# 32 bytes allocated ahead of the arena in a one-layer decoder kernel: every tile behind it moves up by 32 bytes

## What is computed

```python
mod = silu(c) @ w_mod + b_mod                       # 2048 x 12288: six rows or columns of shifts, scales, gates
h = rms_norm(x, norm1_g) * (1 + sc1) + sh1
z = h @ w_in                                        # 2048 x 5296, split into heads, gates, conv channels
o_fox = fox_attention(...)                          # 12 heads of 64
o_nsa = nsa_attention(...)                          # 12 heads, three branches
o_conv = conformer_conv(...)                        # 512 channels, 31 taps
x = x + g1 * (concat(o_fox, o_nsa, o_conv) @ w_out) # 2048 x 2048
h = rms_norm(x, norm2_g) * (1 + sc2) + sh2
x = x + g2 * (relu(h @ w_mlp1) ** 2 @ w_mlp2)       # 2048 x 8192 and 8192 x 2048
return rms_norm(x, final_g)
```

## The kernel before, in words

| tiles | first address | over a multiple of 64 |
|---|---|---|
| `raw`, `w_hi`, `w_lo` | 16,512 | 0 |
| `mod_raw`, `acc`; in them `t_hi`, `t_lo`, `acc_hi`, and `s_hi`, `s_lo` 1 and 2 | 82,048 | 0 |
| small constants and columns (`ident` to `cmp_r`) | 114,816 | 0 or 32 |
| `arena` (68.5 KB): `x_a`, `z_t`, `val_f`, `conv_y`, `mix_f`, `score`, `fox_hi`, `conv_hi`, `x2`, `xn2`, `u_hi`, `u_lo`, `y`, `relu`, `late_raw` | 122,272 | 32 |
| `hold` (32 KB): `act`, `bias_t`, `nsa_hi`, `first_raw` 4 to 6, `end_hi`, `end_lo` | 192,416 | 32 |
| `early3` (4 KB), and at its place `conv_b`, `ones_r`, `s_hi` 0, `s_lo` 0 | 225,184 | 32 |

## Time and profile before

### The profile page before, as it was taken

How to read it: one execution, slowest core, us unless ns; L and a number is a source line. 1 busy time by engine, 2 the same in 40 slices (tenths; PEclk the granted TensorE clock), 3 DMA queues, 4 the chain that set the end, 5 groups by cost and what they waited for, 6 DMA issues and landing times.

```text
span 1172.2 us, 17842 instructions
## 1 busy us (share of the span) xinstructions
PE 1134.7 (97%) x7087; PEld 1005.2 (86%) x7087; DVE 983.7 (84%) x1182; ACT 641.5 (55%) x936; POOL 23.6 (2%) x40
## 2 busy tenths in 40 slices
PE   4999999999999999999999999999999999999996
PEld 4899989999887778999788888888888888888885
DVE  5998989988997988997887788987778987878774
ACT  6655458877775546544454445554455544445452
POOL 1000000100000000010000000000000000000000
PEclk6999999999999999999999999999999999999999
DMA  9999998878966897985657675657674667666451
GB/s 372 420 420 420 421 409 310 255 205 281 358 227 249 301 304 292 401 351 183 210 186 266 240 282 180 215 187 277 238 270 176 218 202 263 251 231 262 152 180 72
DMA packets 48322, 314.65 MB, mean 268 GB/s; under 512 B 6572, under 2 KB 8440, under 8 KB 11768
## 3 DMA queue, kind: packets, MB, share of 16 engines
q1 hardware_dynamic: 44592, 305.72, 70.1%
q0 software_dynamic: 1760, 5.26, 2.4%
q10 hardware_dynamic: 1896, 2.64, 0.8%
HBM read 305.20 MB, written 4.21 MB: 264 GB/s over the span
## 4 chain that ended last, share of the span: by engine, by line
PE 76%; DVE 11%; DMA 5%; ACT 4%; issue 3%; SPq 0%; ACTq 0%; DVEq 0%
PE quad L1285 15%; PE quad L1299 10%; PE quad L1300 10%; PE quad L1301 10%; PE quad L1287 8%; PE quad L1275 5%; PE quad L1276 5%; PE quad L1277 5%; DMA first_raw<-in_w_mod 3%; DVE w_lo L1850 3%; PE quad L1346 2%; PE quad L1345 2%; PE quad L1347 2%; DVE mod_raw L1857 2%; DMA mod_raw<-in_w_mod 2%
## 5 line engine op out<-in xcount | busy, mean ns | idle before, releaser
L893 ACT ACTIVATE w_hi<-raw 128x1024 fp32r<-128x1024 f32 (+1 forms) x342 | 355.4, 1044 | 304.9 <-PE quad L1301 115.9
L1850 DVE TENSOR_TENSOR w_lo<-raw,w_hi 128x1024 fp32r<-128x1024 f32 (+1 forms) x342 | 408.3, 1204 | 112.4 <-ACT w_hi L893 110.4
L1285 PE MATMUL quad<-act,w_hi 128*128 128x512 f32 x768 | 266.4, 390 | 0.0
L1275 PE MATMUL quad<-act,w_hi 128*128 128x256 f32 x760 | 215.2, 283 | 6.0 <-DVE w_lo L1850 3.9
L1287 PE MATMUL quad<-act,w_lo 128*128 128x256 f32 x768 | 216.6, 282 | 0.0
L1276 PE MATMUL quad<-act,w_hi 128*128 128x256 f32 x760 | 213.1, 280 | 0.0
L1277 PE MATMUL quad<-act,w_lo 128*128 128x256 f32 x760 | 213.1, 280 | 0.0
L1285 PEld LDWEIGHTS quad<-act,w_hi 128*128 128x128 f32 x768 | 144.2, 188 | 30.2
L1275 PEld LDWEIGHTS quad<-act,w_hi 128*128 128x128 f32 x760 | 144.1, 190 | 8.7 <-issue 4.6
L1299 PE MATMUL quad<-w_hi,u_hi 128*128 128x512 f32 x376 | 148.8, 396 | 0.6 <-DVE u_lo L2307 0.6
L1301 PE MATMUL quad<-w_hi,u_lo 128*128 128x512 f32 x376 | 148.7, 396 | 0.0
(11 more groups left out here) (371 smaller groups left out, 1715.6 us busy)
## 6 DMA issues: line engine op xcount, KB each, us to landing
raw<-in_w_main SPq DMA_DIRECT2D x184, 1024.0 KB, 5.0
mod_raw<-in_w_mod SPq DMA_DIRECT2D x67, 1024.0 KB, 7.2
first_raw<-in_w_mod SPq DMA_DIRECT2D x14, 1024.0 KB, 15.3
late_raw<-in_w_mod SPq DMA_DIRECT2D x10, 1024.0 KB, 7.9
acc<-in_w_mod SPq DMA_DIRECT2D x4, 1024.0 KB, 12.5
conv_b<-conv_q POOLq DMA_DIRECT2D x8, 512.0 KB, 5.2
x_a<-in_x SPq DMA_DIRECT2D x2, 1024.0 KB, 7.2
x_scratch<-x SPq DMA_DIRECT2D x1, 2048.0 KB, 11.7
```

The source lines that it names most:

```text
L893: A(dst[:, 0:2 * width], block_half(raw, j, width), ACT.Copy).then_inc(hi_done, 1)
L1275: mm(out, hi, act_hi[:, k, :], start=begin and m % 2 == 0, stop=False, skip_group_check=True)
L1285: mm(out, w_hi[j % 4][:, cols], act_both[:, k, :, :].rearrange("p h t -> p (h t)"), start=begin, stop=False, skip_group_check=True)
L1850: TTn(lo[:, 0:2 * width], block_half(raw, j, width), hi[:, 0:2 * width].bitcast(f32), ALU.subtract)\
```

## The change

One tile of 32 bytes per partition is allocated between the small tiles and the arena. Nothing reads or writes it. `arena_at` and `hold_at` are worked out from the allocator's position behind both, and so move with them; `early3` follows.

```diff
         cmp_r = sb("cmp_r", [P, TT * NNSA])
 
 
+        shift = sb("shift", [P, 8])
         arena = sb("arena", [P, ARENA // 4])
         hold = sb("hold", [P, 2 * KT * S])
         arena_at, hold_at = nc.sbuf_base - ARENA - 8 * KT * S, nc.sbuf_base - 8 * KT * S
```

## The result

| kernel | median us | runs | ratio to before | 95% interval |
|---|---|---|---|---|
| before | 1173.41 | 1172.91 to 1174.53, 4 | | |
| changed | 1179.8 | 1176.86 to 1180.97, 4 | 1.0047 | 1.0035 to 1.0058 |
| changed, a second set | 1179.07 | 1178.31 to 1181.45, 5 | 1.0049 | 1.0035 to 1.0062 |

In the second set the kernel before had a median of 1174.06 us. The changed kernel is slower by 5 to 6.4 us; 1181.0 us was forecast. All medians in this document are over executions at the full clock; one execution, the profiled one of e6_arena_minus32, had a granted clock of 0.556 and took 1878.78 us.

A forecast was written before the change was run, and what follows sets the result against it. The prediction took TensorE to bound the kernel. Terms 3.8 + 4.8 + 0.3 - 1.0 = 7.9 us, with the 1172.2 us profiled span and 0.9 us to the median, gave 1181.0 us; 8-in-10 range 1171 to 1186 us.

The forecast's parts named there:

- four signs: Profile after: L1285 at about 396 ns, its pairs 351 to 354, L1275 118 to 119 a matmul, `end_hi` rows at 396.
- What bounds the kernel: Whole kernel: TensorE, busy 97% of the span, hardly waits, so nearly all its lost pace delays the end.
- The pace goes by the moving operand: at a remainder of 32 it is 227 ns: Back-to-back matmuls: moving address 32 over a multiple of 64 gives 227 ns for 512 columns, 0 gives 230 to 233.5.
- The four pairs of remainders: Trace before: bytes over a multiple of 64 for (moving, stationary): (32, 0), (0, 32), (32, 32) and (0, 0).
- the (0, 0) row: Four unread 512-column products, both operands at multiples of 64: read as 230 ns a matmul, to some 3 ns.
- `merged_rows`, +3.8 us: 768 pairs of 512 and 256 columns: from 346.7 to 351.6 ns, 3.8 us more.
- `feature_rows`, +4.8 us less 1.0 hidden: 2280 matmuls of 256 columns: from 116.7 to 118.8 ns, 4.8 us more, 1.0 us of the sum hidden beside other work.
- The last group, +0.3 us: 48 matmuls moving from `end_hi` and `end_lo`: from 227.0 to 233.5 ns, 0.3 us more.
- `token_rows`, 0: Some 1,700 matmuls of 512 columns, only the stationary operand's remainder changing: 0 to 2.9 us, taken as 0.
- VectorE, ScalarE, DMA, 0: Other engines and queues: no cost taken; DMA could be from 2 us less to 2 us more.
- The first rival: Whole kernel: the address's remainder of 64 is not the cause, so no change, 1173.1 us; chance 0.30.
- The second rival: `token_rows`: equal remainders are fast, 1,650 matmuls from 233.3 to 227 ns, 10.4 us less, 1162.7 us; chance 0.12.

The follow-up runs named there:

- e6_arena_minus32: Kernel before with only the arena 32 bytes lower, hold keeping its place: 1168.58 us, ratio 0.9950.
- e2: Kernel before with arena, hold and the tiles behind them 64 bytes higher, instead of the change's 32: 1181.35 us, ratio 1.0070.
- e3: The changed kernel run once more, unaltered, for a second profile: 1179.07 us.
- e10: Kernel before with the arena 32 bytes lower, and `nsa_hi`, `nsa_lo` and `conv_lo` 32 bytes lower within hold: 1168.83 us, ratio 0.9943.
- e4: Kernel before with 32 bytes allocated ahead of the first weight tile, so all those tiles shift and relative places stay: 1173.93 us, ratio 1.0001.
- e5: Kernel before plus 1,248 unread matmuls at 451 us, at 16 relative places in three width sequences: 512 columns took 226.7 to 234.1 ns.
- e9: Kernel before plus blocks of unread 512-column matmuls, varying both operands' places and 128 or 32 stationary columns: 226.7 to 240.1 ns a matmul.
- e1: Kernel before with arena, hold and all behind them 32 bytes lower: 1176.18 us, ratio 1.0019.
- e7: Kernel before with only hold and what lies behind it 32 bytes higher, the arena staying: 1179.35 us, ratio 1.0048.

## Why the prediction was right, and where its steps failed

The direction was right and the range held the time; the reason given for it was wrong, and that the total came within 2 us of the forecast is in part luck. Of the four signs that the prediction named, two came (L1285 at 396 ns, its pairs at 353.3 ns) and two did not (L1275 at 118 to 119 ns a matmul, `end_hi` at 396 ns).

- *What bounds the kernel*: right for the MLP, mostly not for w_in. The first of the unread products at 451 us marks where the MLP begins. In e2 the 1,536 matmuls of `feature_rows` in w_in went from 116.8 to 119.9 ns, 4.8 us in all, and the mark came only 1.3 us later (451.6 for 450.3 us; the four matmuls of the earlier trace rows are the last of six there). In the changed kernel it stands at 450.8 us and in e3 at 451.8. Those 0.5 and 1.5 us can't be given to a cause: in e10, with the places in w_in as before, it is 451.7. From the mark to the end it is 721.9 us before, 724.1 and 726.6 us after. The prediction also has some 200 triples in the first 150 us; there are 240, which makes its 1.3 us 1.5.
- *"The pace goes by the moving operand: at a remainder of 32 it is 227 ns"*: this step failed. The moving operand's own address does not matter (e4), the difference of the two addresses modulo 256 does (e5, e9), with another curve for each sequence of widths. The four pairs of remainders were four points of three curves, and the (0, 0) row, 230 ns, was four matmuls, too few to read a pace from: a block of 24 at place 0 takes 226.7 ns once it has settled (e9's first block), and e5's ninth block took over 228 ns for five steps first.
- *`merged_rows`, +3.8 us*: the term was right in sign and a little small: 353.3 - 346.7 = 6.6 ns x 768 = 5.1 us. The 512 columns gave 5.1 ns, as forecast, the 256 behind them 1.5 ns more, which the forecast left at nothing.
- *`feature_rows`, +4.8 us less 1.0 hidden*: wrong. The pace went to 113.3 or 117.8 ns instead of 118.8, and only the 744 of the MLP count fully: added up there they took 86.6 us before, 84.9 in the changed kernel's first profile (1.7 us less) and 87.4 in e3 (0.8 us more).
- *The last group, +0.3 us*: wrong, 0; it stayed level with `u_hi`.
- *`token_rows`, 0*: right at 233.3 ns, since the curve is flat between 224 and 192.
- *Split products*, not costed: the 270 on u went from 118.2 to 115.1 ns, 0.8 us less, and the 360 on s from 118.6 to 117.7, 0.3 us less; in e3 it is 1.2 us together.
- *VectorE, ScalarE, DMA, 0*: right.

For the second half of the kernel the sum is 5.1 - 1.7 - 1.1 = 2.3 us for the first profile (measured 2.2) and 5.1 + 0.8 - 1.2 = 4.7 us for e3 (measured 4.7). The two paces of `feature_rows` are thus all of the 2.5 us by which these two executions differ there, and the likely part of the changed kernel's wide spread of runs. The same sum works elsewhere: for e1, 6.4 less on u, 5.1 and 2.4 more in pairs and `feature_rows`, 0.8 more in split products, 1.9 us in all (measured 2.0, from 448.8 to 1172.7 us).

The first rival (no change) was wrong as to this kernel, but half of its thought was right: the class of the moved tiles isn't that of 64. The second rival, that equal places are fast, was right for `token_rows`, near the price it named: 5.8 ns a matmul against 6.3, once the places were equal modulo 256 and not modulo 64. The change did not reach that: it went from 224 to 192, away from 0. The reason against it, that `merged_rows` is fast while unequal, was true too; both hold, since each sequence has its own curve.

The rows show no addresses, but the kernel's text gives them, so the difference modulo 256 of each pair of operands could have been worked out beforehand: `end_hi` against `u_hi` (0) beside `w_hi` against `u_hi` (224) was the clean pair.

## What to carry to other kernels

Where fp32r matmuls follow one another without a wait, compare the time from start to start (not the duration) for tiles with different address differences modulo 256 bytes: the pace moved by some 3% with it, and the time of this kernel by 0.5% either way. Place the tiles by the sequence that uses them (here level for 512-column products, 32 bytes apart for 512 and 256 in turn), and measure it: a few blocks of unread matmuls give the whole curve in one run, and one run with everything shifted tells relative from absolute places. Where two tiles differ in more than one remainder, a row that fits a rule on one of them has not shown it.

## What was not expected of the hardware

- The pace of back-to-back fp32r matmuls of 512 columns ranges from 226.7 to 236.7 ns with the two operands' relative address, of period 256 bytes, with no other engine at work; a step of 4 bytes is enough (e9: 226.7 to 236.7).
- It makes no difference where in the partition the two lie: with 32 bytes under everything `token_rows` and the pairs stay within 0.3 ns and the time within 0.1% (e4).
- The same 256-column matmuls at the same addresses have two paces, 113.3 and 117.8 ns at place 64 (the changed kernel, e7) and 116.7 and 117.8 ns at place 32 (e4), and one execution passes from one to the other.
- A stationary operand of 32 columns is not faster than one of 128: 230.5 to 240.1 ns a matmul of 512 columns (e9).
